# Moving a weight-row sum, a split norm pass and attention units in a fused transformer-block kernel

## What is computed

```python
mod = c_act @ w_ada[l] + b_ada[l]
sh1, sc1, g1, sh2, sc2, g2 = [m[:, None, :] for m in jnp.split(mod, 6, axis=-1)]
h = x * (1 + sc1) + sh1
proj = h @ w_in[l]
...                                   # two attentions: ya, yb, then rms_norm each
y = jnp.concatenate([ya, yb], axis=-1) @ w_out[l]
x = layer_norm(DEEPNORM_ALPHA * x + (1 + g1) * y, ln1_g[l], ln1_b[l])
h2 = x * (1 + sc2) + sh2
f = peer_ffn(h2, w_q_peer[l], sub_keys[l], peer_u[l], peer_v[l])
x = layer_norm(DEEPNORM_ALPHA * x + (1 + g2) * f, ln2_g[l], ln2_b[l])
```

## Time and profile before

| what | us |
| --- | --- |
| timed runs, median of 3 | 816.12 (815.91 to 816.32) |
| profiled execution | 814.11 |
| its span in the trace | 812.3 |
| VectorE, TensorE busy | 581.1, 683.8 |
| ScalarE, GpSimd busy | 346.0, 291.3 |

### The profile page before, as it was taken

How to read it: one execution, slowest core, us unless ns; L and a number is a source line. 1 busy time by engine, 2 the same in 40 slices (tenths; PEclk the granted TensorE clock), 3 DMA queues, 4 the chain that set the end, 5 groups by cost and what they waited for, 6 DMA issues and landing times.

```text
span 812.3 us, 7319 instructions
## 1 busy us (share of the span) xinstructions
PE 683.8 (84%) x1988; PEld 325.7 (40%) x1988; DVE 581.1 (72%) x1349; ACT 346.0 (43%) x994; POOL 291.3 (36%) x263
## 2 busy tenths in 40 slices
PE   8999978998999898787989777787878787877785
PEld 4887644554544364443333223222323222222221
DVE  5566968787777987777777878767676757675455
ACT  0013322685575644353545355434343535353333
POOL 1000000344444365554454433443434343434340
PEclk9999999999999999997979999999999999999999
DMA  9999995899999999999999999999999999999993
GB/s 301 379 402 413 416 419 200 356 349 420 392 395 419 422 421 420 421 422 421 420 422 422 419 422 422 420 421 422 422 422 420 422 422 421 422 421 422 421 411 137
DMA packets 57213, 323.74 MB, mean 399 GB/s; under 512 B 6162, under 2 KB 16722, under 8 KB 20946
## 3 DMA queue, kind: packets, MB, share of 16 engines
q0 software_dynamic: 37152, 268.45, 80.0%
q1 hardware_dynamic: 19138, 54.55, 17.5%
q10 hardware_dynamic: 882, 0.27, 0.2%
HBM read 322.18 MB, written 1.07 MB: 398 GB/s over the span
## 4 chain that ended last, share of the span: by engine, by line
DMA 55%; PE 23%; DVE 9%; ACT 6%; issue 4%; SPq 1%; POOL 1%; DVEq 0%; ACTq 0%
DMA ring<-in_experts,e_all 51%; PE bank L529 12%; PE bank L551 4%; DVE ring L882 4%; DMA QT_h2T<-in_w 2%; DMA ring<-in_w 2%; PE bank L601 2%; PE bank L518 2%; ACT diag L728 2%; DVE acc L1038 1%; ACT weight L719 1%; POOL ring L1203 1%; SPq L402 1%; ACT L715 1%; ACT gel L715 1%
## 5 line engine op out<-in xcount | busy, mean ns | idle before, releaser
L529 PE MATMUL bank<-ring,diag 128*128 128x512 f32 x956 | 473.1, 631 | 104.5 <-ACT diag L728 104.3
L1203 POOL DMA_INDIRECT ring<-in_experts,e_all x254 | 282.8, 1113 | 495.1 <-PE bank L529 301.5
L529 PEld LDWEIGHTS bank<-ring,diag 128*128 128x128 f32 x956 | 173.2, 196 | 380.7 <-ACT diag L728 225.8
L882 DVE CUSTOM_DVE_ANT_0 ring<-ring,T_h 128x1024 f32<-128x1024 f32 x128 | 156.7, 1225 | 109.1 <-DMA ring<-in_experts,e_all 109.1
L882 DVE CUSTOM_DVE_ANT_0 ring<-ring,h 128x1024 f32<-128x1024 f32 x128 | 156.6, 1224 | 63.7 <-DMA ring<-in_experts,e_all 61.2
L715 ACT ACTIVATE gel<-pre 128x1 f32<-128x1 f32 x256 | 51.8, 202 | 313.3 <-DVE pre L882 312.5
L728 ACT ACTIVATE diag<-consts,weight 128x128 f32<-128x128 f32 x239 | 95.9, 401 | 7.8
L719 ACT ACTIVATE weight<-gel,g_all 128x1 f32<-128x1 f32 x256 | 75.4, 295 | 9.3
L1038 DVE SCALAR_TENSOR_TENSOR acc<-ring,cact,acc 128x512 f32<-128x512 f32 x56 | 42.1, 752 | 5.4 <-DMA ring<-in_w 3.0
L551 PE MATMUL bank<-hT_yT,lnw 128*128 128x256 f32 x128 | 28.7, 380 | 0.9 <-DVE hT_yT L1003 0.9
L601 PE MATMUL bank<-ring,hT_yT 128*128 128x512 f32 x64 | 28.5, 596 | 0.7 <-DMA ring<-in_w 0.7
(11 more groups left out here) (195 smaller groups left out, 572.9 us busy)
## 6 DMA issues: line engine op xcount, KB each, us to landing
ring<-in_w SPq DMA_DIRECT2D x16, 1024.0 KB, 14.2
H_s<-in_w SPq DMA_DIRECT2D x7, 1024.0 KB, 10.1
ring<-in_w SPq DMA_DIRECT2D x12, 512.0 KB, 10.5
ring<-in_w SPq DMA_DIRECT2D x16, 256.0 KB, 6.5
lnw<-in_w SPq DMA_DIRECT2D x4, 1024.0 KB, 17.7
ring<-in_experts,e_all POOLq DMA_INDIRECT x254, 14.8
H_s<-in_w SPq DMA_DIRECT2D x5, 512.0 KB, 8.2
lnw<-in_w SPq DMA_DIRECT2D x4, 512.0 KB, 8.4
```

The lines of the kernel that those rows point to most:

```text
L529: last = nc.tensor.matmul(tile_sum(t)[n], diag[:, m % DIAGS, :], ring[:, RING_AT[i], D + CH * n:D + CH * n + CH], start=(s == 0), stop=(s ...
L882: nc.vector.tensor_tensor_reduce(ring[:, r, 0:D], ring[:, r, 0:D], h2[i // SLOTS], 1.0, 0.0, ALU.mult, ALU.add, pre[:, i % PAIR:i % PAIR + ...
L1203: nc.gpsimd.indirect_dma_start(ring[:, r, :], None, A["experts"], bass.IndirectOffsetOnAxis(ap=e_all[:, i:i + 1], axis=0)).then_inc(slot_i ...
```

## The change

Four things move; only the split pass alters instructions.

1. In the head of the plan `wsuma 10 0` goes from ahead of `PV 2` and `PV 3` to behind `yT 0 1` and `wo 0 0 1`.
2. The last pass of `ln1b` is done in two halves of 512 columns, each with its own semaphore increment, and each of the two `hT` steps waits for its half alone.
3. In `BESIDE`, `S 4` and `S 5` leave step 0 for steps 2 and 4, so that slots 0 and 1 no longer stand behind both; the other units of the second tile move by some steps up to step 43, and `s 0 3 0` and `s 0 3 1` join in step 68.
4. `NARROW_TO` goes from 12 to 13, so slot 12 also follows its dot by one step.

```diff
-       ("modrow", 4), ("madd", 4), ("Tr", 2), ("Tr", 3), ("wsuma", 11), ("wo", 0, 0, 0), ("wsuma", 10, 0), ("PV", 2), ("PV", 3), ("ny", 0), ("modrow", 5), ("madd", 5),
-       ("yT", 0, 1), ("wo", 0, 0, 1), ("xa", 0), ("wsuma", 10, 1), ("wo", 0, 1, 0), ("rows2",), ("wo", 0, 1, 1), ("ln1a", 0),
+       ("modrow", 4), ("madd", 4), ("Tr", 2), ("Tr", 3), ("wsuma", 11), ("wo", 0, 0, 0), ("PV", 2), ("PV", 3), ("ny", 0), ("modrow", 5), ("madd", 5),
+       ("yT", 0, 1), ("wo", 0, 0, 1), ("wsuma", 10, 0), ("xa", 0), ("wsuma", 10, 1), ("wo", 0, 1, 0), ("rows2",), ("wo", 0, 1, 1), ("ln1a", 0),
...
-NARROW_LAG, NARROW_TO = 1, 12
+NARROW_LAG, NARROW_TO = 1, 13
...
-    0: [("vcopy", 0, 1), ("S", 4), ("S", 5), ("Tr", 4)], 2: [("PV", 4), ("Tr", 5)], 3: [("s", 0, 1, 0), ("s", 0, 1, 1)], 5: [("PV", 5)],
+    0: [("vcopy", 0, 1)], 2: [("S", 4)], 4: [("S", 5), ("Tr", 4)], 5: [("s", 0, 1, 0)], 6: [("PV", 4), ("Tr", 5), ("s", 0, 1, 1)],
...
-                    pe.wait_ge(h2_ready, t + 1)
+                    pe.wait_ge(h2_ready, 2 * t + i + 1)
...
-                    scale(t, h2[t], mod[:, SH2, :], h2[t]).then_inc(h2_ready, 1)
-                    dve.wait_ge(h2_ready, t + 1)
+                    for n in range(2):
+                        half = slice(CH * n, CH * n + CH)
+                        scale(t, h2[t][:, half], mod[:, SH2, half], h2[t][:, half]).then_inc(h2_ready, 1)
+                    dve.wait_ge(h2_ready, 2 * t + 2)
```

## The result

The changed kernel takes **808.29 us** (median of four runs, 807.41 to 809.37) against 816.01 us of the kernel before on the same chip: a ratio of 0.991, interval 0.989 to 0.993. The forecast was 809.0.

A forecast was written before the change was run, and what follows sets the result against it. Transfers bound the kernel, so only an earlier first gather and less starvation can win. 2.2 (start) + 3.9 (first slots) + 1.0 (thinner units) = 7.1 us, from 816.12 to 809.0 us; range 805.3 to 813.6.

The forecast's parts named there:

- What bounds it: Whole kernel: from 230 us transfers run at 423 GB/s; only time without transfers can be won, 8.0 us lost after 160 us.
- Part 1: Head: chunk 10 sums behind the output copies let rows2 start at 119.5 in place of 122.44, 2.9 us earlier.
- Part 2: Last pass of the norm in halves: first transposes start sooner, gaining 0.5 us.
- The gap and the clock: TensorE ahead of the normed tile's transposes: idle of 3.8 us brings 1.2 GHz, costing 1.2 us, ends 0 and 1.5.
- First gather 141.3: Start of the gathers: 2.9 + 0.5 - 1.2 = 2.2 us earlier, at 141.3.
- Part 3: First two slots ahead of the scores: slot 0's place free 5.7 us sooner relative to the stream, 3.9 us recovered.
- 14 us stretch: 160 to 174 us, transfers at only 289 GB/s: 4.4 us lost; 400 GB/s or more expected after the change.
- Part 4: Attention units spread thinner up to slot 40: 1.0 us gained, bounds 3.6 us gone and as much again lost.
- second starved stretch: 204 to 230 us, transfers at 376 GB/s against 423: 2.9 us lost, laid to bursts.
- the full gain: Rival, chance 0.20: clock stays at 2.4 GHz or off the path, both starved stretches go, 804.7 to 808.3 us.
- Slower: Rival, chance 0.06: thin units spoil the ring of six places, 15.9 us lost in place of 8.0, 821.8 us.
- The signs: Right: first gather 140 to 141.5, seventh 153 to 155; wrong: rows2 after 119.6, first gather after 142, rates under 400 GB/s.

The follow-up runs named there:

- twelve traces: One profiled execution each of the kernel before, the changed kernel, its rerun and the variants with parts of the change or additions; their medians run from 807.14 to 820.10 us.
- the two kernels with the old order: Kernel before with the chunk 10 sums moved, without or with the split last pass, BESIDE and NARROW_TO as before: 812.70 and 812.29 us.
- the changed kernel's second trace: The changed kernel, same instructions, run again beside the experiments: 808.94 us, ratio 0.9899 against the kernel before.
- the three others with the old head: Kernel before with only the split last pass, only BESIDE and NARROW_TO changed, or only S 4, S 5, Tr 4 moved to step 2: 814.52, 812.84, 820.10 us.
- order alone: Kernel before with only BESIDE and NARROW_TO as changed, head instructions as before: 812.84 us, ratio 0.9973.
- halves alone: Kernel before with only the last pass of the norm done in two halves, each awaited separately: 814.52 us, ratio 0.9995.
- sums alone: Kernel before with only the two row sums of chunk 10 moved behind the output copies: 812.70 us, ratio 0.9960.
- 1.2 in the three others: Kernel before with moved sums and split pass, without moved units or with units 4 to 7 or 8 to 11 moved: 812.29, 810.03, 814.16 us.
- six traces with the gap open: Changed kernel twice, moved sums without or with split pass, and the latter with units 4 to 7 or 8 to 11 moved: 808.29 to 814.16 us.
- one-step experiment: Kernel before with S 4, S 5 and Tr 4 moved from step 0 to step 2, beside PV 4 and Tr 5: 820.10 us, ratio 1.0037.
- late units alone: Changed kernel with units 4 to 7 put back to their places in the kernel before, units 8 to 11 and later steps moved: 814.16 us, ratio 0.9971.
- the head and the order together: Kernel before with moved sums and split pass only, 812.29 us (0.9960), and with only BESIDE and NARROW_TO changed, 812.84 us (0.9973).

## Why the prediction was right, step by step

- **What bounds it.** Right. The rest of the span is the same within 1.7 us in all twelve traces.
- **Part 1, rows2 2.9 us earlier.** Right: forecast 119.5, measured 119.30 and 119.52 in the two kernels with the old order, 119.84 in the changed kernel's second trace. The wait for ln1 took over, as said. The profiled execution stood at 120.53, likely because of the low clock at 60 us, which no step spoke of. What the step left out is that the old wait brings a low clock of changing length onto VectorE's path: rows2 stood at 122.44 in the trace it read and at 123.59 to 124.10 in the three others with the old head, so the gain is mostly more than 2.9 us.
- **Part 2, 0.5 us.** Right for the start: the wait shrank by 0.54 us, and from rows2 to the first gather it is 21.04 us with the whole pass (kernel before, order alone) and 20.50 with the halves alone. Its worth in time is not resolved.
- **The gap and the clock, 1.2 us with ends of 0 and 1.5.** The mechanism was right, the size only in part. On the path, as the time from the transposes to the first gather over the 10.92 us without a low clock, the price was 2.4 us in the profiled execution, 1.8 in the second trace, 1.7 with the sums alone, and 1.2 in the three others. So 1.2 was met in three of six traces and the upper end of 1.5 was too low for the other three. The price had been taken from one slot or eight long matmuls of before, where the low clock covered only part of the work behind the gap; in the profiled execution both the transposes and most of the q product lay under it. The Trainium skill (TensorE: Matmul & The Clock Gate, "HAM oscillation — how this bites in real kernels") says that work behind a wait of TensorE starts at the lower rate. The six traces with the gap open agree with it.
- **First gather 141.3.** 143.40 in the profiled execution: rows2 was 1.0 us late and the clock 1.2 us dearer. The other traces with this gap have 141.22 to 142.52, late by 0 to 1.2 us.
- **Part 3, seventh gather 5.7 us sooner in the stream, 3.9 us won.** It came 5.5 us sooner, and the loss over the 14 us stretch fell from 4.4 to 0.1 us. But the reason was incomplete: I laid the gain to the two slots in front (only slot 0 stands ahead of all scores), and the one-step experiment shows that this only works when the links of unit 4 stand in separate steps.
- **Part 4, 1.0 us.** Not shown. The late units alone give nothing, and the loss in the second starved stretch goes from 2.8 to 1.4 in the profiled trace while other stretches lose more. Parts 3 and 4 together were to win 4.9 us; the whole loss fell from 9.7 to 5.9, so by 3.8, and only to 8.7 in the second trace.
- **The rivals.** 808.29 also lies at the edge of the span that the full gain was given (804.7 to 808.3); what decides against it is that the clock did fall and the second stretch stayed at 400 GB/s. "Slower" named the right mechanism, a burst that empties the ring, and the one-step kernel made it real: one burst cost a place 10.2 us and the kernel 3 us. I had argued that one burst of 2.65 us cannot empty six places; a chain of dependent links can.
- **The signs.** Of those named for being right, the first gather (140 to 141.5) and the seventh (153 to 155) did not come in the profiled execution, which has 143.40 and 156.05. Two of those named for being wrong did come, rows2 later than 119.6 and the first gather later than 142, in both traces of the changed kernel.

The sum for the profiled execution was 807.0 and came out at 809.37. The 2.4 us are 2.1 of a later start and 1.1 of a smaller gain in lost transfers, less 0.8 in the rest of the span. The medians met, 809.0 against 808.3, and that they met so closely is partly luck: the head was worth more than the trace of before let one see, part 4 cannot be found in the time, and the head and the order together give 1.8 to 2.8 us more than the product of their ratios, with no cause found.

## What to carry to other kernels

When a stream of transfers is the bound, read the kernel as start of the stream plus the time it stands still; two such numbers explained twelve traces to within 2 us. Between the steps that hand buffers back, keep the links of a chain that crosses engines in different steps: one whole attention unit in one step cost 10 us of wait for a buffer. When an edit brings TensorE's work forward by more than VectorE's, look at the gap that opens on TensorE, and price the low clock along the path behind it. And look at more than one trace of the kernel before: a low clock that sits behind a wait there can be the mildest of its kind, and removing the wait is then worth more than the trace says.

## What the runs showed of the hardware

The low clock can fall into the same code in one execution and not in the next: sixteen matmuls at 60 us took 7.11 us in one and 8.80 in another with the same instructions ahead, and behind one and the same wait of about 4.5 us eight matmuls took 4.59, 5.59 and 6.08 us. The kernel before alone ranged from 813.4 to 819.8 us over 35 runs on one chip, which is why parts of 0.5 us were not resolved here. Behind gaps of 3.3 to 4.6 us the transposes took 1.75 to 1.94 us in each of the six traces with the open gap, against 1.04 with the gap filled by 24 matmuls; the product behind them took 4.5 to 5.7 us against 3.81. Of that, 1.2 to 2.4 us reached the first gather.
